# High parts' products first, and one lot of one-hot products inside the tile

## The reference, cut to what matters

```python
s = jnp.einsum('thcd,hcnd->thcn', q, sub_keys, preferred_element_type=f32)
sv, si = lax.top_k(s, PEER_TOPK)
comb = (sv[:, :, 0, :, None] + sv[:, :, 1, None, :]).reshape(T, PEER_HEADS, PEER_TOPK * PEER_TOPK)
cv, ci = lax.top_k(comb, PEER_TOPK)
...
eidx = i1 * PEER_NKEYS + i2
w = jax.nn.softmax(cv, axis=-1)
u = u_tab[eidx]
a = jax.nn.gelu(jnp.einsum('td,thkd->thk', xc, u, preferred_element_type=f32)) * w
return jnp.einsum('thk,thkd->td', a.astype(v_tab.dtype), v_tab[eidx])
```

## Time and profile before

| | us |
|---|---|
| median of 3 runs | 3306.79 |
| lowest and highest | 3304.18, 3309.35 |
| the profiled execution's own time | 3305.77 |
| its span in the trace | 3303.9 |
| PE busy, share of the span | 3011.8, 91% |
| DVE busy, share of the span | 2072.5, 63% |
| ACT busy, share of the span | 1448.4, 44% |

### The profile page before, as it was taken

One profiled execution on the slowest core, in us unless ns is written; L12 is line 12 of the kernel. 1 busy time (PEld: TensorE's weight loads), 2 busy tenths in 40 slices (PEclk: granted clock), 3 DMA queues, 4 the chain that ended last, 5 costly groups with the idle time before them and its releaser, 6 DMA issues.

```text
span 3303.9 us, 54069 instructions
## 1 busy us (share of the span) xinstructions
PE 3011.8 (91%) x18192; PEld 2672.0 (81%) x18192; DVE 2072.5 (63%) x3942; ACT 1448.4 (44%) x2771; POOL 60.7 (2%) x118
## 2 busy tenths in 40 slices
PE   5898988988989779999999999878879999999998
PEld 4678878768879669999997888766679999988886
DVE  3325874438935556887986666323258888966665
ACT  0104433224503243445985555202234448965554
POOL 0000110001100000000000000000000000000000
PEclk8999999989999889999999999986789999999999
DMA  5226874439936135555235555451054553345553
GB/s 159 69 89 197 309 257 127 128 85 337 367 114 183 46 115 172 182 180 171 100 110 184 191 192 195 116 120 34 1 150 165 181 184 121 102 153 193 194 191 120
DMA packets 327611, 519.28 MB, mean 157 GB/s; under 512 B 40673, under 2 KB 231521, under 8 KB 326882
## 3 DMA queue, kind: packets, MB, share of 16 engines
q1 hardware_dynamic: 311106, 457.83, 43.4%
q0 software_dynamic: 16416, 60.30, 5.1%
HBM read 517.02 MB, written 1.05 MB: 157 GB/s over the span
## 4 chain that ended last, share of the span: by engine, by line
PE 81%; DVE 7%; ACT 7%; issue 4%; ACTq 1%; DMA 1%; DVEq 0%; SPq 0%
PE ps L850 29%; PE ps L799 10%; PE ps L801 9%; PE ps L800 9%; PE ps L749 4%; PE ps L779 3%; PE ps L738 2%; PE ps L762 1%; ACT spread L1599 1%; PE ps L1176 1%; ACT spread L1605 1%; PE ps L1298 1%; PE ps L1250 1%; PE ps L1336 1%; ACT hot_pair L1599 1%
## 5 line engine op out<-in xcount | busy, mean ns | idle before, releaser
L799 PE MATMUL ps<-x_high,w_high 128*128 128x256 f32 x3200 | 922.1, 288 | 68.3 <-DVE w_low L1708 49.8
L800 PE MATMUL ps<-x_low,w_high 128*128 128x256 f32 x3200 | 911.0, 285 | 0.0
L801 PE MATMUL ps<-x_high,w_low 128*128 128x256 f32 x3200 | 910.6, 285 | 0.0
L799 PEld LDWEIGHTS ps<-x_high,w_high 128*128 128x128 f32 x3200 | 619.6, 194 | 76.3 <-DVE w_low L1708 53.1
L1751 DVE TENSOR_TENSOR w_low<-tile_ring,w_high 128x512 fp32r<-128x512 f32 x688 | 472.3, 693 | 276.9 <-ACT w_high L1492 184.2
L800 PEld LDWEIGHTS ps<-x_low,w_high 128*128 128x128 f32 x3200 | 620.1, 194 | 0.1
L801 PEld LDWEIGHTS ps<-x_high,w_low 128*128 128x128 f32 x3200 | 619.6, 194 | 0.0
L850 PE MATMUL ps<-w_high,x_high 128*128 128x512 f32 x1376 | 539.8, 392 | 22.6 <-DVE w_low L1751 22.6
L850 PE MATMUL ps<-w_low,x_high 128*128 128x512 f32 x1376 | 539.2, 392 | 0.0
L850 PE MATMUL ps<-w_high,x_low 128*128 128x512 f32 x1376 | 539.0, 392 | 0.0
L1579 ACT ACTIVATE w_high<-tile_ring 128x1024 fp32r<-128x1024 f32 x256 | 269.9, 1055 | 316.7 <-PE ps L801 316.2
(11 more groups left out here) (303 smaller groups left out, 3260.6 us busy)
## 6 DMA issues: line engine op xcount, KB each, us to landing
tile_ring<-peer_u SPq DMA_DIRECT2D x256, 512.0 KB, 3.2
tile_ring<-peer_v SPq DMA_DIRECT2D x256, 512.0 KB, 3.2
arena<-mod_w POOLq DMA_DIRECT2D x112, 512.0 KB, 5.3
tile_ring<-mlp_w_in SPq DMA_DIRECT2D x64, 512.0 KB, 5.1
tile_ring<-mlp_w_out SPq DMA_DIRECT2D x64, 512.0 KB, 5.3
tile_ring<-ret_w_in SPq DMA_DIRECT2D x32, 512.0 KB, 3.8
tile_ring<-peer_w_q SPq DMA_DIRECT2D x32, 512.0 KB, 4.1
ring<-xa_w_kv SPq DMA_DIRECT2D x8, 1024.0 KB, 5.4
```

The lines of the kernel that those rows point to most:

```text
L799: nc.tensor.matmul(dst, w_high[:, a, w_cols], x_high[:, x_chunk, :], start=first, stop=last and bool(kw), **kw)
L800: nc.tensor.matmul(dst, w_high[:, a, w_cols], x_low[:, x_chunk, :], start=False, stop=last and bool(kw), **kw)
L801: return nc.tensor.matmul(dst, w_low[:, a, w_cols], x_high[:, x_chunk, :], start=False, stop=last, **kw)
```

## The change

In every tile the products that need only high parts of the weights come first: 16 of a column tile's 24, 4 of the 6 of a row half. PE now waits for `high_ready` (or `half_high`) ahead of these and for `low_ready` (or `half_low`) ahead of the rest. In the row tiles this needs one more semaphore, `x_cut`, for the low part of the activations, which so far stood ahead of `half_low` in DVE's order; and the two blocks of tokens alternate under each pair of operands. In the tiles that carry tokens lot 2k moves from behind tile k to between its 16 high products and its 8 low ones; lot 2k+1 stays behind the tile. The orders of ACT, DVE and SP are as before, but for the signal of `x_cut`.

```diff
-            def products(dst, w_cols, a, x_chunk, first, last, **kw):
-
-                nc.tensor.matmul(dst, w_high[:, a, w_cols], x_high[:, x_chunk, :], start=first, stop=last and bool(kw), **kw)
-                nc.tensor.matmul(dst, w_high[:, a, w_cols], x_low[:, x_chunk, :], start=False, stop=last and bool(kw), **kw)
-                return nc.tensor.matmul(dst, w_low[:, a, w_cols], x_high[:, x_chunk, :], start=False, stop=last, **kw)
+            def column_products(dst, a, high, low, chunk_ready=None, between=None):
+
+                pe.wait_ge(*high)
+                for c in range(C):
+                    if chunk_ready:
+                        pe.wait_ge(*chunk_ready(c))
+                    cols = w_high[:, a, c * P:(c + 1) * P]
+                    nc.tensor.matmul(dst, cols, x_high[:, c, :], start=c == 0, stop=False)
+                    nc.tensor.matmul(dst, cols, x_low[:, c, :], start=False, stop=False)
+                if between:
+                    between()
+                pe.wait_ge(*low)
+                for c in range(C):
+                    mm = nc.tensor.matmul(dst, w_low[:, a, c * P:(c + 1) * P], x_high[:, c, :], start=False, stop=c == C - 1)
+                return mm
...
-                            if half == 0:
-                                pe.wait_ge(half_low, j * RING + (m0 + k + 1))
-                            else:
-                                pe.wait_ge(low_ready, j * RING + (n0 + k + 1))
-                            for b in range(TB):
-                                for i, (x, w) in enumerate(((x_high, w_high), (x_high, w_low), (x_low, w_high))):
+                            at = j * RING + ((m0, n0)[half] + k + 1)
+                            pe.wait_ge((half_high, high_ready)[half], at)
+                            if half == 0:
+                                pe.wait_ge(x_cut, j * RING + (r0 + k + 1))
+                            for i, (x, w) in enumerate(((x_high, w_high), (x_low, w_high), (x_high, w_low))):
+                                if i == 2:
+                                    pe.wait_ge((half_low, low_ready)[half], at)
+                                for b in range(TB):
...
-                def tile(j, k, begun=True):
+                def tile(j, k, begun=True, between=None):
                     a = k % 2
-                    pe.wait_ge(low_ready, j * RING + (n0 + k + 1))
                     if begun or k >= 2:
                         pe.wait_ge(gate_stored, j * RING + (t0 + k - 1))
-                    for c in range(C):
-                        mm = products(ps[:, 4 + a, 0:T], slice(c * P, (c + 1) * P), a, c, c == 0, c == C - 1)
-                    mm.then_inc(act_sums, 1)
+                    at = j * RING + (n0 + k + 1)
+                    column_products(ps[:, 4 + a, 0:T], a, (high_ready, at), (low_ready, at),
+                                    between=between).then_inc(act_sums, 1)
...
                     for k in range(RING):
-                        tile(j, WEIGH_FROM + k)
-                        for b in range(2):
-                            four_tokens(j, 2 * k + b)
+                        tile(j, WEIGH_FROM + k, between=lambda: four_tokens(j, 2 * k))
+                        four_tokens(j, 2 * k + 1)
...
                     V.tensor_tensor(x_low[:, k % RING, :], src[:, j * RING + k, :], x_high[:, k % RING, :].bitcast(F32),
-                                    ALU.subtract)
+                                    ALU.subtract).then_inc(x_cut, 1)
```

More of the change, by code:

```diff
@@ L358, in build @@
         x_split = sem("x_split")
+        x_cut = sem("x_cut")
         h_squared = sem("h_squared")
@@ L811, in four_units @@
                             pe.wait_ge(unit_taken, j * BANKS + (u0 + q - BANKS + 1))
-                        pe.wait_ge(low_ready, j * (2 * BANKS) + (n0 + k + 1))
-                        for c in range(C):
-                            if early and k == 0:
-                                pe.wait_ge(x_split, earlies.n * C + c + 1)
-                            mm = products(ps[:, (u0 + q) % BANKS, a * T:(a + 1) * T], slice(c * P, (c + 1) * P), a, c,
-                                          c == 0, c == C - 1)
-                        mm.then_inc((tile_used, unit_done)[a], 1)
+                        at = j * (2 * BANKS) + (n0 + k + 1)
+                        chunk_ready = early and k == 0 and (lambda c: (x_split, earlies.n * C + c + 1))
+                        column_products(ps[:, (u0 + q) % BANKS, a * T:(a + 1) * T], a, (high_ready, at), (low_ready, at),
+                                        chunk_ready).then_inc((tile_used, unit_done)[a], 1)
                         if early and k == 1:
@@ L837, in split_token_rows @@
             def split_token_rows(count):
-                n0, m0 = split.n, halved.n
+                n0, m0, r0 = split.n, halved.n, cuts.n
                 def tiles(j, opening=False):
@@ L858, in split_token_rows @@
                 halved.up(count)
+                cuts.up(count)
                 lifts.up()
```

2 lines of the change are left out of this document (1 added, 1 removed).

## The result

| | before | after |
|---|---|---|
| median, us | 3305.48 (4 runs, 3303.98 to 3309.35) | 3332.28 (4 runs, 3327.68 to 3340.95) |
| profiled execution's own time, span | 3305.77, 3303.9 | 3328.05, 3326.2 |
| mean granted clock, share of the full one | 0.950 | 0.957 |

The account below looks back on a forecast made before the run. PE was taken to hold most of the chain, with ACT bounding the token tiles. The terms, 58 - 9.9 - 5.6 - 2.3 - 3.3 = +37, put the median at about 3344 us, 1.1% slower, range 3321 to 3366.

Parts of the forecast that it names:

- Part 1: Tiles that carry tokens: the even lot inside the tile lengthens rounds from 5.18 to 6.08 us, +58 us for both layers.
- the ring: In the token tiles, ACT's even rows, lot, low products and ACT's next `high` follow in turn: 6.08 us a round.
- the last three rounds: End of an expert layer's lots: rounds of 4.90 us before take 5.94, 3 x 1.04 = 3.1.
- Rival 3: Token tiles: PE's clock falls to its lower level, 3457 us (5%); after only the first tile's stop, 2 to 4 us.
- Part 2: Column tiles elsewhere: PE's waits for low parts go; MLPs -9.9, expert layers' starts -5.6, stick-breaking and retention starts -2.3.
- More than the stop, so I take all of them away: MLP column tiles: the first low product comes 1.92 us behind the tile's start, so all `w_low` stops vanish, -9.9.
- rival 4: MLPs: the stops only move, to ACT or the loads, so 10 us of gain are missing, 3354; 15%.
- both first tiles: First column tiles of the two MLPs: they wait for chunks of activations, which the change leaves, so 0.
- The starts of the expert layers: PE no longer waits for `w_low` behind DVE's residual work and starts earlier: -2.8, twice, -5.6.
- The idle time ahead of stick-breaking and retention: Both streams' starts lose one `w_low` wait, 1.1 to 1.2 long each: -2.3 in all.
- Part 3: Row tiles: half a tile's subtraction leaves PE's path at six stream starts, 6 x 0.6, of which 3.3 is taken.

Follow-up runs that it names:

- ACT's other order: The changed kernel with ACT writing a tile's even rows ahead of `high` and the gelu, not behind them: 3277.31 us, ratio 0.9928, round 5.148.
- the shifted: The kernel before with ten useless small float32 products on TensorE ahead of the second cross attention: 3297.67 us, ratio 0.9991.
- the fastest kernel: The changed kernel with both lots behind the tile, MLPs' first column tiles in old order, ACT's `Abs` of both lots before both `Relu`: 3249.04 us, ratio 0.9829.

## Why the prediction was right

**Part 1, +58.** The mechanism is shown from both sides: the lot alone brings the loss, taking it back removes it, halving the work behind the wait takes off that half, and ACT's other order opens the ring. The term by its parts, for one round:

| | predicted | measured |
|---|---|---|
| `high` to the even rows' end | 3.64 | 3.64 |
| to the lot's start | 0.23 | 0.24 |
| the lot | 0.91 | 0.90 |
| 8 low products, then ACT's `high` | 0.92 + 0.38 | 1.23 |
| round | 6.08 | 6.02 |
| each of the last three rounds | 5.94 | 5.95 |

A layer's lots, from the first to the row stream, cost +27.9 and +27.1 us where 28.5 stood (29.0 less the row start). The round's missing 0.06 us lies in the last item: the end of a tile reaches ACT some 0.07 sooner than in the row that I read it from the earlier trace rows.

**Rival 3** holds for the first tile of each layer only: its stop of 1.92 us is followed by a lot at the lower level (1.84 us long, not 1.15; in the second layer it is the odd lot, 1.91; the mean clock of the 5 us around them is 0.81 and 0.66), and in the windows of the loop none of the shorter stops is. The prediction had "about 1.9" for that stop. The Trainium skill (TensorE: Matmul & The Clock Gate, "A second HAM failure mode: psum-queue depth-cycling") tells of a kernel in which short idle times between groups of matmuls made the clock swing. In this loop, with 1.11 us of idle time in each 6.02, the granted clock is 1.00 from 1560 to 1700 us, so it does not swing here.

**Part 2, -9.9 for the MLPs: the step that failed.** "More than the stop, so I take all of them away" was right for DVE's waits, and wrong for the second MLP's time: with the loads halved the stage gains 6.2 us, with them whole 0.8. It is in the main rival 4, the stops moved to the loads, which I gave 15%; the windows before show the loads' share at 1.03 in that very stretch, and I had not asked for it. And both first tiles cost +1.15 that I had at 0, as PE works at the lower clock for twice as long; with their old order the second MLP gains 3.9 at whole loads. The starts of the expert layers came as forecast, 14.71 to 11.84 us of idle time, -2.87 against -2.8; behind them comes what I had not counted: the mean clock of the first layer's first 5 us is 0.62 instead of 0.50 and 1.00 in the next 5 instead of 0.94. By the end of the query tiles, 49 us on, this layer is 0.9 us ahead and the second 0.2. By the first lot they are 1.9 and 1.3 ahead; a stop of 0.19 on `w_low` is gone on the way, and the rest I can't place. The idle time ahead of stick-breaking and retention fell by 6.78 - 5.92 = 0.86 and 6.47 - 5.16 = 1.31, against 1.15 each.

**Part 3, -3.3.** The row starts lost 0.6 each (the second from 2.38 to 1.78), and the order within a tile shows no price: the same 443 products in the 100 us from 1900, before and after. As a term for these starts it was right; for what the new row order does to the time it was far too small, -12.9 by its own runs, and the difference goes with a higher clock.

**What the sum had no term for** is the granted clock in work that the change leaves as it was: -1.1, -5.0, -3.5, and -10.4 + 2.8 = -7.6 of the stage from 1737.2, together -17. The -5.0 comes back in eight of the nine profiles with the new row tiles; of the others each varies by some us between profiles. By stages, the second MLP with its first tile came out 6.3 above its terms, the first MLP 1.4 above, the two expert layers' columns 5.1 below (1.9 and 1.3 us ahead of the first lot, the rest for the lots), and the others together at the terms: 37 + 6.3 + 1.4 - 5.1 - 17 is 22.6, and the pair shows 22.3. The forecast stood 12 us above the median of the runs. So the mechanism that sets the sign was right, and its size too: the lots cost 55 of the 57 us forecast for them. That the smaller misses of 8 on the one side and 22 on the other partly cancel is luck.

## What to carry to other kernels

Before moving a wait ahead on one engine, list what stands behind it, and who waits for that: if the engine that is waited for waits itself for something behind the wait, the two take turns, and the round is their sum (6.02 us) instead of the longer of the two (5.18). A stop that is removed is only worth what the next resource allows, so look at the loads' share of that stretch first. And where an engine waits for its own result once per group, gather two groups: that gave 24 us here.

## What the runs showed of the hardware

- **The clock.** The same instructions with the same pauses ran at different levels in different kernels: the fall at 680 us, which cost some 5 us in the kernel before, is absent in the shifted and in the changed one, and the stage from 1737 us took 685.4 us in one profile and 675.6 in the other. The time at the lower level was 328 to 339 us in four profiles with the old row tiles and 284 to 311 in nine with the new. So an edit can be worth several us (here some 8 of 12) in instructions that it doesn't touch. And runs of one kernel differ by as much: of the kernel before, runs of 3295 to 3297 us had a mean clock of 0.952 or 0.953, and those of 3305 us and more mostly 0.949 to 0.951.
- **The one-hot lots.** A lot that PE had to wait for takes 0.90 to 0.91 us until the next product starts, an even one right behind a tile 0.89, and an odd one that follows a lot without a wait 0.81. So the round without stops is 4.65; the 4.90 of the written-out rounds before was not PE's own need.
- **DVE and ACT at full share.** In the fastest kernel all three engines are busy for 97 to 100% of the loop at once, and their instructions take the same within 2%: `high` 1.06 us there and in the changed kernel, three `Relu` 1.25 and 1.26, `w_low` 1.226 and 1.220 on average.
